# Dilated attention's values in blocks of 512 columns, two tiles at a time, and linear attention three plan steps sooner

## The reference, cut to what matters

```
nx = rmsnorm(h, attn_norm_g[l])
proj = jnp.einsum('bsd,dp->bsp', nx, w_in[l])
gq, gk, gv, gr, glow, dq, dk_, dv_ = jnp.split(proj, split_at, axis=-1)
...
o_a = gla_mixer(gq, gk, gv, glog)            # heads split out
o_a = o_a * lax.rsqrt(jnp.mean(o_a * o_a, axis=-1, keepdims=True) + EPS)
o_a = o_a * gla_norm_g ... * jax.nn.silu(gr.astype(jnp.float32))
o_b = dilated_mixer(dq, dk_, dv_, rel_bias)
mixed = jnp.concatenate([o_a, o_b], axis=-1).astype(h.dtype)
h = h + jnp.einsum('bsm,md->bsd', mixed, w_out[l])
```

## Time and profile before

| | |
|---|---|
| Time, median of 3 runs | 1360.12 us (1359.04 to 1360.42) |
| The profiled execution's own time | 1359.01 us |
| Its span, first to last instruction | 1357.6 us |
| DVE busy | 877.6 us (65%) |
| ACT busy | 818.7 us (60%) |
| POOL busy | 336.1 us (25%) |
| Instructions | 19539 |

### The profile page before, as it was taken

One profiled execution on the slowest core, in us unless ns is written; L12 is line 12 of the kernel. 1 busy time (PEld: TensorE's weight loads), 2 busy tenths in 40 slices (PEclk: granted clock), 3 DMA queues, 4 the chain that ended last, 5 costly groups with the idle time before them and its releaser, 6 DMA issues.

```text
span 1357.6 us, 19539 instructions
## 1 busy us (share of the span) xinstructions
PE 1347.0 (99%) x7510; PEld 1135.5 (84%) x7510; DVE 877.6 (65%) x1548; ACT 818.7 (60%) x1235; POOL 336.1 (25%) x306
## 2 busy tenths in 40 slices
PE   9999999999999999999999999999999999999999
PEld 6977956789899898887778888888888898889889
DVE  6055466678576673357798889965447785568557
ACT  6575566663544535666587777775656645753653
POOL 0211101235343251111211211211113261315214
PEclk9999999999999999999999999999999999999999
DMA  7976643925426137877655585767898546825723
GB/s 251 242 166 142 149 117 76 230 36 193 104 90 183 29 136 187 189 167 155 144 128 128 131 216 125 145 150 171 206 225 193 105 139 178 180 47 165 190 50 109
DMA packets 57969, 202.45 MB, mean 149 GB/s; under 512 B 6450, under 2 KB 7019, under 8 KB 57748
## 3 DMA queue, kind: packets, MB, share of 16 engines
q0 software_dynamic: 25632, 93.09, 36.8%
q1 hardware_dynamic: 31380, 106.24, 23.8%
q10 hardware_dynamic: 864, 1.87, 0.4%
HBM read 199.05 MB, written 2.12 MB: 148 GB/s over the span
## 4 chain that ended last, share of the span: by engine, by line
PE 78%; DVE 12%; ACT 6%; issue 2%; DMA 2%; SPq 0%; DVEq 0%; POOL 0%; ACTq 0%
PE bank L660 19%; PE bank L667 18%; PE bank L664 18%; PE bank L698 17%; DVE eb L1730 2%; PE bank L813 1%; DVE eb L1725 1%; ACT zs L1152 1%; PE bank L885 1%; ACT WL L1038 1%; ACT WH L1030 1%; DVE zb L1745 1%; DMA WL<-in_w_gu 1%; DVE zb L1733 1%; DMA RAW<-in_w_in 1%
## 5 line engine op out<-in xcount | busy, mean ns | idle before, releaser
L660 PE MATMUL bank<-NH,WH 128*128 128x512 f32 x1152 | 459.9, 400 | 0.5 <-ACT NH L1207 0.2
L667 PE MATMUL bank<-NH,WL 128*128 128x512 f32 x1152 | 448.0, 390 | 0.6 <-DVE WL L1465 0.3
L664 PE MATMUL bank<-NL,WH 128*128 128x512 f32 x1152 | 448.0, 390 | 0.6 <-DVE NL L1470 0.5
L660 PEld LDWEIGHTS bank<-NH,WH 128*128 128x128 f32 x1152 | 216.5, 188 | 60.5 <-issue 18.7
L667 PEld LDWEIGHTS bank<-NH,WL 128*128 128x128 f32 x1152 | 216.3, 188 | 47.1 <-DMA WL<-in_w_gu 0.9
L664 PEld LDWEIGHTS bank<-NL,WH 128*128 128x128 f32 x1152 | 216.7, 188 | 44.8 <-DVE NL L1470 1.6
L1030 ACT ACTIVATE WH<-RAW 128x1024 fp32r<-128x1024 f32 (+3 forms) x148 | 151.9, 1031 | 74.4 <-PE bank L667 39.2
L698 PE MATMUL bank<-AH,WH 128*128 128x256 f32 x644 | 182.5, 283 | 0.3 <-DVE AL L2113 0.3
L698 PE MATMUL bank<-AL,WH 128*128 128x256 f32 x644 | 182.2, 283 | 0.0
L698 PE MATMUL bank<-AH,WL 128*128 128x256 f32 x644 | 182.2, 283 | 0.0
L1038 ACT ACTIVATE WL<-WH 128x1024 fp32r<-128x1024 f32 (+1 forms) x146 | 153.1, 1050 | 11.2 <-DMA WH<-in_w_in 8.9
(11 more groups left out here) (375 smaller groups left out, 2120.9 us busy)
## 6 DMA issues: line engine op xcount, KB each, us to landing
WL<-in_w_in POOLq DMA_DIRECT2D x58, 512.0 KB, 6.8
RAW<-in_w_gu SPq DMA_DIRECT2D x44, 512.0 KB, 5.2
WL<-in_w_gu POOLq DMA_DIRECT2D x34, 512.0 KB, 7.8
RAW<-in_w_ff SPq DMA_DIRECT2D x32, 512.0 KB, 4.8
WH<-in_w_in POOLq DMA_DIRECT2D x32, 512.0 KB, 6.5
RAW<-in_w_in SPq DMA_DIRECT2D x28, 512.0 KB, 5.9
quarters<-in_w_ff SPq DMA_DIRECT2D x24, 512.0 KB, 4.7
WL<-in_w_ff POOLq DMA_DIRECT2D x17, 512.0 KB, 6.3
```

Of the source, the lines that this page charges most:

```text
L660: e.matmul(o, a[0], a[1], start=(k == 0), stop=False)
L664: e.matmul(o, b[0], b[1], start=False, stop=False)
L667: mm = e.matmul(o, c[0], c[1], start=False, stop=(k == t.kt - 1))
```

## The change

vD becomes one unit of 512 columns with its own array of weights, `w_vd`, and four tiles. The tiles go in two pairs. Within a pair, the first two channel steps of one tile come first, then those of the other, then steps 2 to 5 of both alternate, and the last two steps of each follow apart. The stage still counts for 32 plan steps. The read-out of vD copies 512 columns at once, four times in place of eight. `T_D` is three steps smaller, which moves every generator of linear attention and the transfers tied to it. The gate temporaries lie in rows 4 and 5 of `mixed`, which hold the one-hot matrices until the two band products are made and are written by the dilated attention only later; `decay` waits for no gate any more.

```
--- before.py
+++ after.py
@@ -134,7 +134,7 @@
         add("gG", "w_in", 3, 5, 8, UC)
         add("qD", "w_in", 5, 7, 8, UC)
         add("kD", "w_in", 7, 9, 8, UC)
-        add("vD", "w_in", 9, 11, 8, UC)
+        units.append(("vD", "w_vd", None, 8, 512, 0))
         add("wo0", "w_out", 0, 2, 4, 512)
         add("wo1", "w_out", 2, 4, 4, 512, 4)
         for g in range(4):
@@ -198,7 +198,7 @@
                     first = self.together[-1][0]
                     t.v0, first.v1 = first.v0, v - 1
                     self.together[-1].append(t)
-                elif st == "vS" and c:
+                elif st == "vS" and c or st == "vD" and c % 2:

                     self.together[-1].append(t)
                 else:
@@ -206,6 +206,9 @@
             if st == "vS":
                 for n, t in enumerate(mine):
                     t.v0, t.v1 = v - 32 + 2 * n, v - 2 * (NT - 1 - n)
+            if st == "vD":
+                for first, second in (mine[0:2], mine[2:4]):
+                    second.v0, first.v1 = first.v0, second.v1 - 2
             for p in range(self.first[u], self.first[u + 1]):
                 _, k, m = self.pieces[p]
                 self.used[p] = t.v0 + (t.v1 - t.v0) * (k + m) / kt
@@ -219,7 +222,7 @@
                     yield tiles[0], n, None
                 continue
             kt = tiles[0].kt
-            many = len(tiles) > 2
+            many = len(tiles) > 2 or tiles[0].st == "vD"
             if many:
                 for t in tiles:
                     for k in (0, 1):
@@ -496,7 +499,7 @@

             return s % 2 if bank == 0 else bank + 1

-        T_D = plan.start("qD")
+        T_D = plan.start("qD") - 3.0
         T_A1, R1 = plan.start("wo0"), 3 * 0.71
         T_A2, R2 = plan.start("hq") - 10.0, 4 * 2.3
         T_H, R3 = plan.start("gs"), 3.5
@@ -1069,7 +1072,7 @@
                     act.wait_ge(("product", "tile", t.g), ("scale_columns", ph))
                     if st == "vS" or st == "vH":
                         act.wait_ge(*second_end)
-                    n = min(t.cols, S if st == "vS" else UC)
+                    n = min(t.cols, S if st in ("vD", "vS") else UC)
                     o = e.activation(v[:, j, c * n:(c + 1) * n], bank[:, 0:n], ACT.Copy, scale=rcol[:, j:j + 1])
                     if st == "vG" and c == 0:
                         e.activation(glN[:, 16 * j:16 * j + 16], bank[:, UC:UC + 16], ACT.Copy,
@@ -1396,7 +1399,8 @@

             streams = [prologue(), ones(), splits(), negated(), root("attn", mean_time["attn"]), columns("attn", 30.0)]
             streams += [natural("vG", vG, "attn"), natural("vD", vD, "attn")]
-            streams += silu_gates("gG", lambda i: mixed[:, i, :], gt_, lambda i: [("gate", "gG", i - 2)] if i >= 2 else [])
+            streams += silu_gates("gG", lambda i: mixed[:, i, :], [mixed[:, 4, :], mixed[:, 5, :]],
+                                  lambda i: [("gate", "gG", i - 2)] if i >= 2 else [("band", i)])
             streams += [gla(0), gla(1)]
             streams += [mixed_split("mixed", k, T_A1 - 2.0 + 0.2 * k, [("gla_out", k), ("product", "block", plan.last_unit("vD"), k)])
                         for k in range(4)]
@@ -1610,11 +1614,11 @@
                     e.tensor_tensor(halves(x, m)[1], halves(d, m)[1], halves(qc, m)[1], ALU.mult).then_inc(*dve.sig("gla_x", c, m, 1))

                 yield gla_time(c, 5) + 0.1
-                decay(64, B64, d0, [("gla_out", 1)] if c else [("gate", "gG", 2)])
+                decay(64, B64, d0, [("gla_out", 1)] if c else [])
                 yield gla_time(c, 6)
                 values(64, d0, x64, [("gla_64", 0, 1)] if c else [])
                 yield gla_time(c, 7) + 0.1
-                decay(128, B128, d1, [] if c else [("gate", "gG", 3)])
+                decay(128, B128, d1, [])
                 yield gla_time(c, 8)
                 values(128, d1, x128_, [("gla_128", 0, 1)] if c else [])
                 dve.wait_ge(("gla_x", c, 64, 1))
@@ -2139,7 +2143,8 @@

             streams = [prologue(), early_low(), sums("attn"), root("attn", mean_time["attn"]), bands(), low_rank()]
             streams += [put("qG", qG, 0.125), put("kG", kG)]
-            streams += silu_gate("gG", lambda i: mixed[:, i, :], lambda i: g_gla[:, i:i + 1], gt_, [])
+            streams += silu_gate("gG", lambda i: mixed[:, i, :], lambda i: g_gla[:, i:i + 1],
+                                 [mixed[:, 4, :], mixed[:, 5, :]], [])
             streams += [gla(0), gla(1), put("qD", qD, 0.125), put("kD", kD)]
             streams += [mixed_split("mixed", k, T_A1 - 2.0 + 0.2 * k, []) for k in range(4)]
             streams += [dilated(), to_h("wo0", "wo0", lambda k: x_in(k)[-1])]
@@ -2403,7 +2408,8 @@
     a = {"c_f32": f, "c_masks": u, "onehot": oh}
     w_in = x["w_in"][0]
     x_t = x["x"][0].T.reshape(8, P, S).transpose(1, 0, 2).reshape(P, 8 * S)
-    a["w_in"] = cut(np.concatenate([w_in[:, 0:512], w_in[:, 768:1536], w_in[:, 1552:3088]], 1), 8, UC)
+    a["w_in"] = cut(np.concatenate([w_in[:, 0:512], w_in[:, 768:1536], w_in[:, 1552:2576]], 1), 8, UC)
+    a["w_vd"] = cut(np.ascontiguousarray(w_in[:, 2576:3088]), 8, 512)[0]
     a["w_vg"] = cut(np.concatenate([w_in[:, 512:768], w_in[:, 1536:1552]], 1), 8, UC + 16)[0]
     wo = x["w_out"][0]
     a["w_out"] = cut(wo, 4, 512)
```

## The result

The changed kernel takes 1362.83 us, the median of 8 runs (1361.98 to 1367.22), against 1359.39 us of the kernel before, also 8 runs (1358.76 to 1360.49): a ratio of 1.0029, 95% interval 1.0020 to 1.0037. That is 3.4 us slower (interval 2.7 to 5.0 us). The prediction had set 2.72 us as the least difference that it would call slower; the median is beyond that, the lower end of the interval only just reaches it. I had given that outcome 17% and "same" 80%. The forecast was 1361.3 and its range, 1358.6 to 1363.4, holds the median. Run again in a later comparison, the same kernel took 1362.14 us (9 runs, 1361.71 to 1365.93) against 1359.67, a ratio of 1.0021, interval 1.0011 to 1.0031.

The account below looks back on a forecast made before the run. TensorE, at work 99%, was taken as the bound. -1.28 + 1.82 + 0.34 + 0.46 = +1.34 us gave 1360.35 on the profiled execution, 1361.5 on the median; forecast 1361.3, own range 1360.0 to 1362.8, 8 in 10 1358.6 to 1363.4.

Parts of the forecast that it names:

- Term 1: vD on TensorE: 96 matmuls of 512 columns replace 192 of 256, saving 1.28 us.
- Term 2: First head pair of linear attention: helpers don't get sooner, line 766 starts 0.60 late, line 793 1.82 us late in all.
- The removed waits for gates 2 and 3 win nothing: Decay in the first head pair: no gain, since exponentials and scans end later than those gates.
- Term 3: Head 0's normalisation: a qD read-out moves into the chain ahead of head 1's sum, costing 0.34 us, between 0 and 0.68.
- The second head pair: Linear attention's second pair: an added kD read-out and rounded piece move nothing on TensorE, 0 us, at most 0.68.
- Term 4: Start of wo0: operand rows come late behind pieces 29 to 31, costing 0.46 us, between -0.25 and 1.0.
- Term 5: Piece 29 behind the first scores: low weights land 0.4 us late, absorbed by existing idle time, cost 0.
- The rival of the late piece: Piece 29's low weights land 2.7 us late, 1.6 beyond what is absorbed: 1363.0 us; 18%.
- the pair keeps pace: First head pair: ACT or DVE are in time, no TensorE wait there or at head 1's sum: 1359.3 us; 22%.
- The wide matmuls save what they should: Answers the rival for vD that wide matmuls save next to nothing, making Term 1 0: 1362.6 us; 3%.

Follow-up runs that it names:

- two waits put back: Kernel before with gate temporaries in `mixed`, plus long-met waits for gates 0 and 1 at the decay's steps for levels 64 and 128: 1359.66 us, ratio 1.0000.
- the rows ahead of piece 31: Changed kernel with wo0's four operand rows NH rounded ahead of piece 31's two steps instead of behind them: 1362.91 us, ratio 1.0019.
- the second trace: Profiled execution of the changed kernel's repeat, no edit, granted clock 1.000; the repeat's median is 1362.14 us.
- the first trace: Profiled execution of the changed kernel in the first comparison, no further edit: 1367.22 us, mean granted clock 0.996.
- the other half alone: Kernel before with `T_D` three steps sooner, temporaries in `mixed`, no waits for gates 2 and 3, values still in 256 columns: 1365.73 us, ratio 1.0034.
- one step: Wide values with wo0's rows ahead of piece 31, plus linear attention one step sooner and gate 3's read-out right behind its product: 1360.83 us, ratio 1.0008.
- the wide values: Changed kernel with linear attention and gate temporaries put back as before, leaving vD in four tiles of 512 columns: 1360.07 us, ratio 0.9999.

## Why the prediction was right or wrong

**What bounds the kernel: right.** TensorE is at work 99% of either trace, and what the traces show of the change is the distance of matmuls, idle stretches of TensorE, and its clock.

**Term 1, the matmuls (-1.28): right.** From 169.41 to 171.90 lie 11 matmuls, 0.2264 us each; 96 of them are 21.73 us, against 23.04 of the earlier trace rows: 1.31 saved. The 0.24 us worked out from the formula of the Trainium skill (TensorE: Matmul & The Clock Gate, "Back-to-back issue gap") is not what the rows show: 226.4 ns against 120.0, so two narrow matmuls cost 13.6 ns more than a wide one, not 2.5. The section gives the formula for an isolated matmul and says itself that it doesn't fit a stream, which the prediction passed over; its own figure for a stream of 512 columns, some 131 ns, isn't what this trace has either.

**Term 2, the first head pair (+1.82): right in size and cause, wrong in one place, and without its sequel.** From 759 to 796 the lag grows by 0.15 + 1.67 = 1.82 us. The read-out of gate 3 was forecast for 84.60 and stood at 84.92 in a trace that is 0.37 late; 769 came 0.66 late instead of 0.60. The rest was forecast whole at 796, and 0.48 of it falls at 790, which waits for its bank until the masked copies (1630) are through. The experiment with the read-out moved up shows the cause: with gate 3's work out of the way of `gX` the stalls are gone. What the prediction lacked is that the clock can fall behind stalls this close together: 7.12 - 2.37 = 4.75 us more in the trace that shows it. The forecast is 1.5 below the median of all eight runs, and 0.9 below that of the five whose clock stayed (1362.21).

**"The removed waits for gates 2 and 3 win nothing": right** for the first head pair. In every trace with it, but for the one with two waits put back, TensorE waits 0.5 us more near the end of the program, over a thousand microseconds later, which no row around the change could show.

**Term 3, head 0's normalisation (+0.34): right kind, mis-sized.** The wait is 0.61 us and the lag grows by 0.55, within the bounds of 0 and 0.68. I had let DVE's own latency hide 0.2 us of the added read-out. Without that the sum is 0.68 - 0.15 = 0.53, so it hid nothing.

**The second head pair (0): right.** Its first line, 769 at 137.00, is 0.70 behind the kernel before, as head 1's sum was.

**Term 4, wo0's start (+0.46): right, a little low.** wo0 was due 0.23 behind the last matmul, at 172.13; ACT's first row NH starts at 171.78 (E - 0.35, forecast E - 0.4); from E to the first scores it is 2.40 us (forecast 2.3, before 1.84), thus 0.56. The remedy that suggests itself fails, as Term 5 explains.

**Term 5, piece 29 (0): right.** Its transfer goes out at 168.09, E - 4.04, and its weights are used at 177.02, 8.9 us after the issue. That is a wait of 0.90 us, and the transposes still start 5.30 us behind the scores, as before (5.29): all of it is absorbed. The rival of the late piece would have begun to cost just there; the experiment with the rows ahead of piece 31 pushed it over the edge.

**The sum.** Forecast +1.34 up to the first transposes; measured 2.17 - 0.37 = 1.80, so 0.46 above; Terms 3 and 4 are 0.31 of that, the rest is spread over lines with no wait of their own. Behind them the second trace loses 0.6 us by 601 us, 1.0 at line 888 and 0.5 near the end. The last is tied to the temporaries; the other two are not explained, and the repeat's median, 1.1 below its profiled run, says that not every run has them.

So the mechanism of each term held, and the change as a whole was forecast too small: +1.34 us, against 2.8 in the five undisturbed runs of the first comparison, 3.4 in all eight and 2.5 in the repeat. That the forecast lies as near as 1.5 is in part luck, since it was put on 1360.12, the median of three runs, and the kernel before measured 1359.39.

**The rivals.** That the pair keeps pace was wrong for this order of instructions and comes true with gate 3's work moved: 1359.96 us, where that rival had 1359.3. The wide matmuls save what they should. The late piece did not decide. The chance for "slower", 17%, was too low: it held the misses of single terms and no stretch in which the kernel could lose what the terms don't name.

## What to carry to other kernels

Moving a chain sooner is worth nothing while what feeds it, here gate 3's read-out and activations, stays in place: look at which instruction of the moved chain meets an unmoved one on the same in-order engine. A wait of TensorE is not priced by its length alone when others stand close to it: the clock can fall behind a cluster of waits that are short each. And a saving on TensorE buys time only if what must be ready at its end was ready early: here 1.3 us of matmuls were given back at head 3's sum and at wo0's rows.

## What the runs showed of the hardware that was not expected

**The clock falls behind clustered stalls.** In the first trace TensorE was at work for 1.79 of 2 us and then 1.24 of 2 us, with no single wait above 0.6 us in the rows, and its clock went from the 2.4 to the 1.2 GHz level for 10 us. It is not certain: the second trace has 1.05 of 2 us in the same place and kept its clock. Of the kernels with such stalls, 5 of 17 runs of the changed kernel, 4 of 6 with the other half alone, 6 of 12 with the rows moved and 4 of 11 with one step have a mean clock below 1.000. Of the 67 runs of the six kernels without them one has, the profiled one of the wide values, and of the kernel before 3 of 80 and the one at 1894.66. Single longer waits go ahead of a fall too: the 1.68 us in the kernel with the rows moved and the 2.10 us in that of the wide values. What a fall costs isn't the same each time: of the kernel with one step, the four runs with a lower clock took 1361.91 to 1364.48 us, where others took 1358.53 to 1360.83. No run put such stalls in on purpose, so it is seen that a fall comes behind them, not shown that they cause it, and why it comes only sometimes stays open.

**DVE beside POOL.** A subtraction of 128x512 with both inputs in SBUF took 0.69 us alone and 1.43 to 1.78 us where POOL's additions had begun ahead of it (1.43, 1.73 and 1.78 in three traces). Where the subtraction had begun first, by 0.06, 0.21 and 0.50 us in three traces, it took 0.69 although POOL's addition ran beside it. So it seems to matter which engine begins; POOL's times are rough, and no run tested that alone. In the kernel before POOL's sum met line 939 instead (1.57 us at 264.54), where nothing waited.

**With two waits that are always met put back, a stall of 0.5 us that lies 1250 us behind them was gone.** Seen in one comparison of traces, as told above; that the waits are the cause isn't settled.
